# State-space group norm: how the reciprocal roots reach the partitions, and when the group is scaled

## The reference, cut to what matters

```python
y = y.reshape(bsz, length, D_SSD) * jax.nn.silu(z.astype(f32))
yg = y.reshape(bsz, length, SSD_GROUPS, D_SSD // SSD_GROUPS)
yg = yg * lax.rsqrt(jnp.mean(yg * yg, axis=-1, keepdims=True) + RMS_EPS)
return (yg.reshape(bsz, length, D_SSD) * norm_w.astype(f32)).astype(z.dtype)
```

## Time and profile before

| | us |
|---|---|
| median of three runs | 1692.39 |
| the profiled execution | 1692.11 |
| its span | 1690.3 |
| PE busy | 1668.8 |
| DVE busy | 1331.9 |
| ACT busy | 980.2 |
| GpSimd busy | 68.2 |
| DMA, moved | 308.11 MB, mean 182 GB/s |

### The profile page before, as it was taken

The page is one execution under the profiler, slowest core; times in us unless marked ns, Lnnn a source line. Parts: engine busy times, 40 slices in busy tenths (PEclk is TensorE's granted clock), DMA queues, the critical chain, the costliest instruction groups (busy, mean ns, idle before and its releaser), DMA issues.

```text
span 1690.3 us, 27093 instructions
## 1 busy us (share of the span) xinstructions
PE 1668.8 (99%) x10712; PEld 1483.7 (88%) x10712; DVE 1331.9 (79%) x2070; ACT 980.2 (58%) x1628; POOL 68.2 (4%) x81
## 2 busy tenths in 40 slices
PE   8999999999999999999999999999999999999997
PEld 7999888888999988888899889888889988988886
DVE  5867678888877758888889998766678999886666
ACT  5577556665757656656644875544454477554442
POOL 1100000000200000000000011000000000100001
PEclk9999999999999999999999999999999999999999
DMA  6666555555556646555465544655646645466652
GB/s 217 188 198 175 187 173 182 194 194 167 175 174 189 188 160 205 191 190 199 151 214 186 166 172 159 215 185 190 196 142 218 215 139 176 149 208 191 199 194 80
DMA packets 237484, 308.11 MB, mean 182 GB/s; under 512 B 6483, under 2 KB 198701, under 8 KB 237357
## 3 DMA queue, kind: packets, MB, share of 16 engines
q1 hardware_dynamic: 237049, 306.26, 56.8%
q10 hardware_dynamic: 308, 0.12, 0.0%
HBM read 301.04 MB, written 1.11 MB: 179 GB/s over the span
## 4 chain that ended last, share of the span: by engine, by line
PE 83%; DVE 12%; ACT 3%; issue 1%; POOL 1%; ACTq 0%; DVEq 0%; POOLq 0%
PE ring_banks L540 62%; PE bank L540 17%; DVE weights_lo L1611 4%; DVE conv_sums L2034 3%; PE bank L819 1%; ACT weights_hi L1176 1%; PE bank L928 1%; POOL small L1079 0%; PE bank L827 0%; PE bank L779 0%; DVE norm_statistics L1740 0%; PE bank L939 0%; PE bank L742 0%; ACT decay L1263 0%; DVE residual L2299 0%
## 5 line engine op out<-in xcount | busy, mean ns | idle before, releaser
L1611 DVE TENSOR_TENSOR weights_lo<-raw_weights,weights_hi 128x1024 fp32r<-128x1024 f32 (+1 forms) x550 | 642.9, 1209 | 98.4 <-ACT weights_hi L1176 97.1
L540 PE MATMUL ring_banks<-input_parts,weights_hi 128*128 128x256 f32 (+1 forms) x4000 | 691.8, 325 | 5.9 <-ACT input_parts L1214 2.2
L1176 ACT ACTIVATE weights_hi<-raw_weights 128x1024 fp32r<-128x1024 f32 (+1 forms) x552 | 544.2, 1036 | 193.8 <-PE ring_banks L540 97.3
L540 PEld LDWEIGHTS ring_banks<-input_parts,weights_hi 128*128 128x128 f32 x4000 | 592.8, 190 | 68.5 <-issue 10.0
L540 PE MATMUL ring_banks<-input_parts,weights_lo 128*128 128x256 f32 x2752 | 373.7, 283 | 0.0
L540 PEld LDWEIGHTS ring_banks<-input_parts,weights_lo 128*128 128x128 f32 x2752 | 356.6, 191 | 7.3
L540 PE MATMUL bank<-weights_hi,hidden_hi 128*128 128x512 f32 x432 | 110.7, 392 | 0.0
L540 PE MATMUL bank<-weights_hi,hidden_lo 128*128 128x512 f32 x432 | 109.3, 389 | 0.0
L540 PE MATMUL bank<-weights_lo,hidden_hi 128*128 128x512 f32 x432 | 109.3, 389 | 0.0
L2034 DVE SCALAR_TENSOR_TENSOR conv_sums<-conv_padded,params_second_layer,conv_sums 128x256 f32<-128x256 f32 x240 | 98.7, 476 | 0.0
L540 PEld LDWEIGHTS bank<-weights_hi,hidden_lo 128*128 128x128 f32 x432 | 81.1, 188 | 16.9
(11 more groups left out here) (262 smaller groups left out, 1715.5 us busy)
## 6 DMA issues: line engine op xcount, KB each, us to landing
raw_weights<-in_w_in SPq DMA_DIRECT2D x104, 1024.0 KB, 5.3
raw_weights<-in_w_ff SPq DMA_DIRECT2D x64, 1024.0 KB, 5.4
raw_weights<-in_w_ffn_up SPq DMA_DIRECT2D x44, 1024.0 KB, 5.1
raw_weights<-in_w_ffn_down SPq DMA_DIRECT2D x22, 1024.0 KB, 4.9
raw_weights<-in_w_out SPq DMA_DIRECT2D x16, 1024.0 KB, 5.3
squares<-decay_rows SPq DMA_DIRECT2D x16, 512.0 KB, 4.7
raw_weights<-in_w_o SPq DMA_DIRECT2D x8, 1024.0 KB, 5.1
pair<-pair SPq DMA_DIRECT2D x64, 64.0 KB, 2.9
```

What stands on the lines that cost most here:

```text
L540: return mm(o, w, x, start=first, stop=last, skip_group_check=True)
L1176: A(whi[:, t, i * n:(i + 1) * n], raw[:, s, i * n:(i + 1) * n], ACT.Copy).then_inc(hi_done, 1)
L1611: tt(wlo[:, t, r], raw[:, s, r], whi[:, t, r].bitcast(f32), SUB).then_inc(w_ready, 1)
```

## The change

The reciprocal roots no longer go through diagonal matrices and TensorE. GpSimd, after its power, stores the 128 by 2 roots in a DRAM tensor in the order of the tokens, waits for the store, and loads the 256 values from there as one row into each of the 128 partitions, into the first two of the eight slices of the tile `diagonals`. `group_spread`, `root_diagonals` and their semaphores are gone. DVE scales from that row in SBUF. The scaling with its high and low part stands one iteration later: in `extras(c + 3)`, that is in iterations 17, 21, 25 and 29 where it was in 16, 20, 24 and 28. From the second group on, the load also waits until the group before is scaled, since the row has one buffer.

```diff
+        root_rows = diag[:, 0:2, :].rearrange("p a b -> p (a b)")
+        root_store = nc.dram_tensor("group_roots", [DEPTH, GROUPS, TOK, P], f32).ap()
...
-                def group_spread(g):
-                    b = acc[2 + g % 2]
-                    pe.wait_ge(gdiag, l * 4 + g + 1)
-                    for t in range(TOK):
-                        last = mm(b[:, t * P:(t + 1) * P], K("ones"), diag[:, t, :], start=True, stop=True)
-                    last.then_inc(gbc, 1)
...
-                    if c - 2 in GROUP_END:
-                        group_spread(GROUP_END[c - 2])
...
+            def group_rows(k):
+
+                spread_roots(k, TOK)
+                pool.wait_ge(spread_root, k + 1)
+                store = root_store[k // GROUPS, k % GROUPS]
+                fetch(nc.gpsimd, store.rearrange("t p -> p t"), small[:, 24:24 + TOK], roots_stored)
+                pool.wait_ge(roots_stored, 16 * (k + 1))
+                if k:
+                    pool.wait_ge(y3_ready, k)
+                rows = store.rearrange("t p -> (t p)").unsqueeze(0).to_broadcast([P, SEQ])
+                nc.gpsimd.dma_start(root_rows, rows).then_inc(root_rows_loaded, 16)
...
-                spread_roots(k, TOK)
+                group_rows(k)
...
-                    if c - 2 in GROUP_END:
-                        group_hi(GROUP_END[c - 2])
+                    if c - 3 in GROUP_END:
+                        group_hi(GROUP_END[c - 3])
...
-            def root_diagonals(k, n, signal):
-
-                y = small[:, 24:24 + n]
-                dve.wait_ge(spread_root, k + 1)
-                for i in range(n):
-                    last = ts(diag[:, i, :], ident, y[:, i:i + 1], None, MUL)
-                last.then_inc(signal, 1)
...
-                    rsqrt_diagonals(l * 4 + g, acc[2 + g % 2][:, 0:TOK], TOK, 1.0 / 256, gdiag)
+                    ask_roots(acc[2 + g % 2][:, 0:TOK], TOK, 1.0 / 256)
...
-                    dve.wait_ge(gbc, l * 4 + g + 1)
+                    dve.wait_ge(root_rows_loaded, 16 * (l * 4 + g + 1))
                     for m in range(2):
                         k = 2 * g + m
-                        last = stt(out=yb[:, m, :], in0=yb[:, m, :], scalar=p1("ssd_norm", k), in1=acc[2 + g % 2][:, 0:SEQ], op0=MUL, op1=MUL)
+                        last = stt(out=yb[:, m, :], in0=yb[:, m, :], scalar=p1("ssd_norm", k), in1=root_rows, op0=MUL, op1=MUL)
...
-                    if c - 2 in GROUP_END:
-                        group_scale(GROUP_END[c - 2])
-                    if c - 2 in GROUP_END:
-                        group_lo(GROUP_END[c - 2])
+                    if c - 3 in GROUP_END:
+                        group_scale(GROUP_END[c - 3])
+                        group_lo(GROUP_END[c - 3])
```

More of the change, by code:

```diff
@@ L321, in build @@
         exp_ready, v_ready, y_done = sem("exp_ready"), sem("decayed_ready"), sem("y_done")
-        y2_ready, gsq_ready, gstat, gdiag, gbc = sem("y2_ready"), sem("gsq_ready"), sem("gstat"), sem("gdiag"), sem("gbc")
+        y2_ready, gsq_ready, gstat = sem("y2_ready"), sem("gsq_ready"), sem("gstat")
+        roots_stored, root_rows_loaded = sem("roots_stored"), sem("root_rows_loaded")
         y3_ready, y_hi, mixssd_ready = sem("y3_ready"), sem("y_hi"), sem("mixssd_ready")
@@ L1639, in ask_roots @@
                 ts(small[:, 16:16 + n], sums, scale, EPS, MUL, ADD).then_inc(spread_var, 1)
-            def root_diagonals(k, n, signal):
-                y = small[:, 24:24 + n]
-                dve.wait_ge(spread_root, k + 1)
-                for i in range(n):
-                    last = ts(diag[:, i, :], ident, y[:, i:i + 1], None, MUL)
-                last.then_inc(signal, 1)
-            def rsqrt_diagonals(k, sums, n, scale, signal):
-                ask_roots(sums, n, scale)
-                root_diagonals(k, n, signal)
             def root(r, t, centred):
```

## The result

The changed kernel took 1735.14 us in the median of 4 runs (1731.16 to 1738.19), the kernel before 1692.43: the ratio is 1.0249, with a 95% interval of 1.0233 to 1.0266. It is 43 us slower. The forecast was 1693.7 and its range ended at 1700.5; rival 1 ("the roots come late") was right in kind, with a price of 8 us where some 41 came.

The account below looks back on a forecast made before the run. TensorE, busy 1668.8 of 1690.3 us, was taken as the bound. Spreads gave -3.8 us and later scaling 2 x 2.5, transfers being in time: +1.3, making 1693.7 us, range 1689.0 to 1700.5.

Parts of the forecast that it names:

- rival 1: The roots come late for the scaling: round trip 14 us, 4.0 per layer, 8 in all, 1701.7 us; chance 0.20.
- the two rows of the same route: Kernel before's store of running sums to DRAM, 4.8 us, and load spreading such rows over partitions, 4.7; basis for the round trip.
- The last row: Profile row of the kernel before, taken as transfers of small pieces, landing 3.6 to 9.8 us after issue.
- the two bounds, 7.2 and 19.6: Round trip of the roots, store plus load, as 2 x 3.6 and 2 x 9.8 us.
- the limits: Time available for the roots' round trip: 11.3 us in group 3, 11.5 in group 2, 14 in groups 0 and 1.
- The sum: Spreads' gain of 3.8 us against added PE waits of 2.5 per layer: +1.2 to +1.3 us, 1.3 taken.
- the spreads: Removing TensorE's spread products gives PE back 0.47 us each, 3.8 us for 8 spreads.
- the diagonals: Two DVE instructions and a wait leave iterations 15, 19, 23 and 27; counted 0, as DVE then waits for ACT's split.
- the walk through ACT and DVE: Scaling one iteration later: PE waits 1.4 us more before norm(1), 0.6 before norm(2), 0.5 before chunk 31, per layer.
- Rivals 2 and 3: 2: the full 2.16 us passes on, 1697.7, chance 0.13; 3: ACT and DVE take up the delay, 1689.6, chance 0.20.
- I count nothing for the time they take: Four 128 KB row loads in a layer are half of one weight load; time taken from it counted as nothing.
- The port rule: GpSimd is kept from writing its transfers' descriptors while VectorE holds their shared ports; would make the roots late.

Follow-up runs that it names:

- Run 9: Changed kernel with the roots stored as 128 pieces of 8 bytes instead of 256 of 4, DVE reading with a step of two: 1700.69 us, ratio 1.0049.
- run 2: Changed kernel without its sixteen transfers; one row from an input, loaded once at the start, scales all groups instead of their roots: 1697.62 us, ratio 1.0025.
- run 3: Changed kernel without its transfers, plus products of zeros before the norm products of group 1 (six) and group 2 (two): 1693.92 us, ratio 1.0009.
- run 10: Changed kernel with products of zeros in TensorE's stands: 28 and 18 before group 1's norm product, 2 before group 2's, 30 in the last chunks: 1732.91 us.
- run 5: Kernel before, with only GpSimd's 256-piece store of the roots added and read by nobody: 1695.31 us, ratio 1.0018.
- run 4: Kernel before, with GpSimd's store and row load of the roots made beside it, read by nobody; diagonals and spreads stay: 1702.38 us, ratio 1.0057.
- run 7: Changed kernel with both transfers issued by SyncE between the loads of weights instead of by GpSimd: 1725.86 us, ratio 1.0196.
- run 8: Kernel before with three rounds of four GpSimd probe transfers, while weights stream and after the last output; 256-piece store 8.4 us quiet, kernel time of no interest.
- run 12: Version without transfers or diagonals: a full matrix of ones puts sums on every partition, ACT takes roots, scaling in its old place: 1696.73 us, ratio 1.0022.

## Why the prediction was wrong

- **Failed: "I take 4.8 + 4.7 plus 0.3 for the waits = 9.8 us, the sum of the two rows of the same route."** It is 10.3 + 6.3 and the hand-over between them, 14.3 to 20.7 us from the roots to the scale. The rows chosen had the same route but another shape: the store of the running sums is 16 KB in long rows. No row of before had the shape of 256 pieces of 4 bytes. The last row, which the forecast read as small pieces, is of loads alone, and its 9.8 us is one load of 16 KB spread over 128 partitions among the first transfers of the program. So that the two bounds, 7.2 and 19.6, nearly held the truth is partly luck; but they did say that the limits could be missed. Run 9 shows that the shape alone is 34 us.
- **Too small: rival 1's price.** It put 14 us into the round trip and found 8 us in all. With 20.0 in group 0 and 18.9 in group 3 its own rule gives 6.0 and 7.6 us of stand, and they are 5.8 more (7.18 against run 2's 1.40) and 7.5 more. The limits fit these two groups, in the second layer too (2.9 and 6.9 us over, 2.7 and 7.3 more). In groups 1 and 2 some 2.5 to 3 us more were hidden: 4.1 and 6.7 us over 14 became 1.0 and 4.2 more in group 1, 3.9 and 2.8 over 11.5 became 1.06 and nothing in group 2.
- **Left out: the clock behind a stand.** The sum counted a stand at its length. 1.4 us of standing cost 1.5 more (run 2), and filling the stands gives 3.0 us back by the traces and 2.9 to 3.7 by the times (run 3). In the changed kernel slower matmuls make 15 to 16 of the 46.0 us, but run 10 shows that only some 5 of them could be had back alone: the others lie in stretches whose pace the roots set.
- **Left out: what the transfers do to others.** "I count nothing for the time they take" looked at 128 KB of row loads. The 1 KB store is what slows the weights and `decay_rows` (run 5), 2.3 us alone and 9.4 with the row load behind it (run 4), in a kernel that is otherwise the one before. In the changed kernel ACT never waits for `decay_rows` and only 1.2 us, once, for a load of the layers' input weights, against 1.0 before. So this error is a real one but doesn't make the 43 us.
- **Right: the spreads, the diagonals, the walk through ACT and DVE.** Run 2 puts the norm product at 147.4 against 147.5, and its waits at 1.40, 0.54 and 0.35 against 1.7, 0.6 and 0.5. Rivals 2 and 3 are out with it. That run 3 then has 1693.9 for the case that the forecast described confirms the walk, not the forecast of this change.
- **The port rule** that the forecast cited from the Trainium skill (SBUF — State Buffer, "Who interferes with whom") led to the right rival by a cause that the runs don't bear out: with SyncE as the issuer, the store takes as long (10.5 us against 10.3, run 7). The estimate from the Trainium skill's page DMA: Bandwidth & Descriptors, "Anatomy of one DMA" (2.0 us and the bytes over 436 GB/s), would be 2.0 us for the store, where a quiet chip takes 8.4 in 256 pieces.

## What to carry to other kernels

Price a transfer by the number and size of its pieces on either side, and look for a row of that shape rather than of the same route; if only bounds are to be had, put each bound through the schedule's limits before choosing, as here 11.3 us of slack met a range from 7.2 to 19.6. Before moving work later for a transfer, price the move with the transfer free: here that alone ate more than the products it saved. And a stand of TensorE can be paid a second time through its clock (1.4 us was here, 0.54 wasn't), if TensorE sets the pace behind it.

## What the runs showed of the hardware

- A store of 1 KB in 256 pieces of 4 bytes landed after 8.3 to 8.6 us with nothing else moving, in 128 pieces of 8 bytes after 3.3 to 3.7, and a single piece of 8 bytes after 1.5 to 1.6 (run 8).
- While such a store was on its way, a load of 1 MB issued behind it on another queue moved at 0 to 59 GB/s instead of 372 to 392 and landed after 11.7 us instead of 5.3; one issued 1.7 us ahead of the store landed after 5.4 as without it. Three such loads landed after 8.4 us in the median instead of 5.4 (run 5).
- Small transfers suffer from the stream in turn: one piece of 8 bytes took 6.8 us in the median instead of 1.5, the row load 4.9 (run 8) to 6.3 (the changed kernel) instead of 3.2.
- The granted clock was still 0.50 for five microseconds of full work after a stand of 7.2 us, and a stand of 1.4 us was enough for it to average 0.66 between 150 and 155 us (run 2). A stand of 0.54 us left it at 1.00.
- A table load of ScalarE took 1.28 us, and 16 more of them came with eight square roots between other functions (run 12).
